# Entry of the gate/up product: x scaled, rounded and split tile by tile, the first three pieces taken by k

## What is computed

```python
x = x + gt_m * (merged @ w_out[l])

h = rms_norm(x, g_ffn_norm[l]) * (1.0 + sc_f) + sh_f
g_ff, u_ff = jnp.split(h @ w_gate_up[l], 2, axis=-1)
x = x + gt_f * ((jax.nn.silu(g_ff) * u_ff) @ w_down[l])
```

## Time and profile before

| | |
|---|---|
| median of 3 runs | 1420.42 us (1415.7 to 1421.6) |
| profiled execution | 1419.05 us |
| its span | 1417.0 us |
| PE busy | 1224.0 us, 86% of the span |
| DVE busy | 921.1 us, 65% |
| ACT busy | 414.4 us, 29% |

### The profile page before, as it was taken

The page is one execution under the profiler, slowest core; times in us unless marked ns, Lnnn a source line. Parts: engine busy times, 40 slices in busy tenths (PEclk is TensorE's granted clock), DMA queues, the critical chain, the costliest instruction groups (busy, mean ns, idle before and its releaser), DMA issues. The chain is left out here.

```text
span 1417.0 us, 20158 instructions
## 1 busy us (share of the span) xinstructions
PE 1224.0 (86%) x7886; PEld 834.8 (59%) x7886; DVE 921.1 (65%) x2035; ACT 414.4 (29%) x882; POOL 276.2 (19%) x264
## 2 busy tenths in 40 slices
PE   4897998878887888888887777889999989899998
PEld 1887867533332424333332222358999669799998
DVE  1594336698787968788786865665556656555542
ACT  2551215311110111111010010244454354544431
POOL 0000000045344444444343444400000000000000
PEclk9899999989999999999999999999999999999999
DMA  9366079599999999999999999973443764344552
GB/s 395 144 238 186 3 282 428 225 408 423 422 420 421 422 421 420 417 419 420 421 400 423 421 401 421 422 316 120 179 170 128 314 280 179 120 179 179 183 207 117
DMA packets 50766, 428.33 MB, mean 302 GB/s; under 512 B 5744, under 2 KB 7920, under 8 KB 8304
## 3 DMA queue, kind: packets, MB, share of 16 engines
q0 software_dynamic: 36864, 268.45, 45.9%
q1 hardware_dynamic: 13808, 158.59, 28.8%
HBM read 423.64 MB, written 1.05 MB: 300 GB/s over the span
## 5 line engine op out<-in xcount | busy, mean ns | idle before, releaser
L1407 PE MATMUL bank<-arena 128*128 128x512 f32 x1024 | 497.1, 614 | 107.3 <-DVE arena L1577 106.8
L1407 PEld LDWEIGHTS bank<-arena 128*128 128x128 f32 x1024 | 176.6, 190 | 408.3 <-DVE arena L1577 271.1
L530 PE MATMUL bank<-rounded,rounded 128*128 128x256 f32 x1288 | 381.0, 296 | 35.6 <-DVE rounded L489 20.6
L1639 DVE CUSTOM_DVE_ANT_0 arena<-arena 128x1024 f32<-128x1024 f32 x256 | 313.4, 1225 | 140.4 <-DMA arena<-experts_in,arena 139.2
L1321 POOL DMA_INDIRECT arena<-experts_in,arena x256 | 275.6, 1077 | 611.6 <-PE bank L1407 352.1
L531 PE MATMUL bank<-rounded,rounded 128*128 128x256 f32 x1288 | 370.6, 288 | 0.0
L532 PE MATMUL bank<-rounded,ring_r 128*128 128x256 f32 x1288 | 369.7, 287 | 0.0
L507 DVE TENSOR_TENSOR ring_r<-ring,rounded 128x1024 fp32r<-128x1024 f32 (+2 forms) x155 | 194.8, 1264 | 143.9 <-ACT rounded L502 142.9
L530 PEld LDWEIGHTS bank<-rounded,rounded 128*128 128x128 f32 x1288 | 252.8, 196 | 44.6 <-issue 32.6
L531 PEld LDWEIGHTS bank<-rounded,rounded 128*128 128x128 f32 x1288 | 252.8, 196 | 3.3 <-issue 2.9
L532 PEld LDWEIGHTS bank<-rounded,ring_r 128*128 128x128 f32 x1288 | 252.9, 196 | 0.0
(11 more groups left out here) (254 smaller groups left out, 946.3 us busy)
## 6 DMA issues: line engine op xcount, KB each, us to landing
ring<-slots_in SPq DMA_DIRECT2D x68, 2048.0 KB, 8.7
arena<-slots_in SPq DMA_DIRECT2D x4, 2048.0 KB, 23.4
arena<-experts_in,arena POOLq DMA_INDIRECT x256, 13.6
xT<-xT_in SPq DMA_DIRECT2D x1, 1024.0 KB, 10.9
mixT<-slots_in SPq DMA_DIRECT2D x1, 1024.0 KB, 13.7
out_dram<-xT SPq DMA_DIRECT2D x1, 1024.0 KB, 3.9
arena<-slots_in SPq DMA_DIRECT2D x1, 896.0 KB, 12.6
uT<-arena SPq DMA_DIRECT2D x4, 142.0 KB, 9.5
```

The costliest lines, as they stand in the source:

```text
L530: pe.matmul(dst, hi[:, k, :], xh, start=(k == 0), stop=False)
L1407: ins = pe.matmul(psum[2 * tt + half][:, :], diag[:, r % DIAGS, :], rows[:, r % GRING, D + 512 * half:D + 512 * half + 512], start=(h == 0 ...
L1639: dve.tensor_tensor_reduce(rows[:, r % GRING, 0:D], rows[:, r % GRING, 0:D], utok[:, tt, :], 1.0, 0.0, ALU.mult, ALU.add, hdot[:, r:r + 1] ...
```

## The change

The third weight split moves from behind the loop of the block before into iteration 4, with the two others behind it. In the gate/up block ACT writes the rounded tile straight from the scaled tile with the shift as its bias, and DVE makes the low part in one operation, (scaled + shift) - rounded, two tiles behind the scaling. The count of low parts rises by one for a tile (eight, where it was four), for which `Split.xcount` is raised by four more. PE takes pieces 0 to 2 together: for each tile k three matmuls for each of the three pieces, into three banks. Later pieces no longer wait for x.

```diff
--- before.py
+++ after.py
@@ -1196,13 +1196,11 @@
                         act.preload_act_table_set("natural_log_exp_and_others")
                     for i in range(len(tiles)):
                         sp3.act_hi(act, i + LEAD)
-                        if following and i in (5, 6):
-                            following.act_prime(act, i - 5, i - 4)
+                        if following and i in (4, 5, 6):
+                            following.act_prime(act, i - 4, i - 3)
                         if squares:
                             act.wait_ge(ev, i + 1)
                             act.activation(uT[:, i, :], xT[:, i, :], ACT.Square).then_inc(nm_sq, 1)
-                    if following:
-                        following.act_prime(act, 2)
 
                 @block.vector
                 def _(dve):
@@ -1214,8 +1212,8 @@
                         sp3.dve_prime(dve, 1)
                     for i, (s, _) in enumerate(tiles):
                         sp3.dve_lo(dve, i + LEAD)
-                        if following and i in (5, 6):
-                            following.dve_prime(dve, i - 5, i - 4)
+                        if following and i in (4, 5, 6):
+                            following.dve_prime(dve, i - 4, i - 3)
                         dve.wait_ge(mm, i + 1)
                         dve.scalar_tensor_tensor(xT[:, i, :], psum[i][:, 0:T], gates[:, i:i + 1], xT[:, i, :],
                                                  ALU.mult, ALU.add).then_inc(ev, 1)
@@ -1223,8 +1221,6 @@
                             dve_add_square(dve, i - 1)
                         if i == len(tiles) - 1 or tiles[i + 1][0] != s:
                             dve.sem_inc(slot_used[(s0 + s) % RING], 1)
-                    if following:
-                        following.dve_prime(dve, 2)
             parts[0] += 1 if squares else 0
 
         eight = [(i // 4, (i % 4) * P) for i in range(8)]
@@ -2148,6 +2144,7 @@
         residual_block("o2", "w_out2", eight, merged, mod2[:, 16:24], (after("w_br"), after("w_out2")), 0, split=o2,
                        following=wgu)
         ffn2_norm = Norm(gain[:, 3, :], mod2[:, 24:32])
+        Split.xcount += KT // 2
         down = residual_split("dn", "w_down", [(i, 0) for i in range(8)], FT, ff, DOWN_AT - 3 * FT * P, width=P, buffers=4,
                               x_split=(ffh, ffl), turn=3)
         with nc.Block() as block:
@@ -2157,18 +2154,32 @@
 
             @block.tensor
             def _(pe):
-                for n in range(4 * NGU):
+                pe.wait_ge(split_lo, wgu.base + LEAD)
+                for k in range(KT):
+                    pe.wait_ge(split_xlo, wgu.xbase + k + 1)
+                    for n in range(LEAD):
+                        hi, lo, dst = wgu.part(n), wgu.weights(n, True), psum[n][:, 0:T]
+                        pe.matmul(dst, hi[:, k, :], wgu.xh[:, k, :], start=(k == 0), stop=False)
+                        pe.matmul(dst, hi[:, k, :], wgu.xl[:, k, :], start=False, stop=False)
+                        ins = pe.matmul(dst, lo[:, k, :], wgu.xh[:, k, :], start=False, stop=(k == KT - 1))
+                        if k == KT - 1:
+                            ins.then_inc(gu_mm, 1)
+                for n in range(LEAD, 4 * NGU):
                     s, j = n // 4, n % 4
                     if s >= 2:
                         if j < 2:
                             pe.wait_ge(gu_act, 2 * (s - 2) + j + 1)
                         else:
                             pe.wait_ge(gu_ev, 2 * (s - 2) + j - 1)
-                    wgu.pe_products(pe, n, psum[n % 8][:, 0:T]).then_inc(gu_mm, 1)
+                    wgu.pe_products(pe, n, psum[n % 8][:, 0:T], wait_x=False).then_inc(gu_mm, 1)
 
             @block.scalar
             def _(act):
-                ffn2_norm.act(act, wgu)
+                ffn2_norm.act_rstd(act)
+                for k in range(KT):
+                    act.wait_ge(nm_n, KT * ffn2_norm.n + k + 1)
+                    act.activation(wgu.xh[:, k, :], uT[:, k, :], ACT.Identity,
+                                   bias=ffn2_norm.shifts[:, k:k + 1]).then_inc(split_xhi, 1)
                 for m in range(4 * NGU):
                     s, j = m // 4, m % 4
                     wgu.act_hi(act, m + LEAD)
@@ -2187,7 +2198,19 @@
 
             @block.vector
             def _(dve):
-                ffn2_norm.dve(dve, wgu)
+                def lower_part(k):
+                    dve.wait_ge(split_xhi, wgu.xbase + k + 1)
+                    dve.scalar_tensor_tensor(wgu.xl[:, k, :], uT[:, k, :], ffn2_norm.shifts[:, k:k + 1], wgu.xh[:, k, :],
+                                             ALU.add, ALU.subtract).then_inc(split_xlo, 1)
+
+                dve.wait_ge(nm_rstd, 2 * ffn2_norm.n + 2)
+                for k in range(KT):
+                    dve.scalar_tensor_tensor(uT[:, k, :], xT[:, k, :], ffn2_norm.gains[:, k:k + 1], ffn2_norm.root,
+                                             ALU.mult, ALU.mult).then_inc(nm_n, 1)
+                    if k >= 2:
+                        lower_part(k - 2)
+                lower_part(KT - 2)
+                lower_part(KT - 1)
                 for m in range(4 * NGU):
                     s, j = m // 4, m % 4
                     wgu.dve_lo(dve, m + LEAD)
```

## The result

| | before | after |
|---|---|---|
| median | 1420.42 us (5 runs, 1415.38 to 1421.6) | 1410.94 us (5 runs, 1407.86 to 1413.56) |
| ratio | 1 | 0.9933, 95% interval 0.9906 to 0.9959 |
| profiled execution | 1419.05 us | 1408.15 us |
| its span | 1417.0 us | 1406.1 us |

A forecast was written before the change was run, and what follows sets the result against it. The prediction took the gate/up and down stages to be bound by PE. Savings of 1.2, 2.2 and 0.5 us sum to 3.9, giving 1416.5 us against the median, range 1412.8 to 1420.0.

The forecast's parts named there:

- Part 1: End of the block before: without the third weight split in its tail, the logarithm comes earlier, 1.2 us saved.
- Part 2: Gate/up entry: x made tile by tile brings the first matmul 1.83 us behind the first scaling, 2.2 us saved.
- Part 3: Behind PE's stop before gate/up: half clock lasts 3.4 us instead of 4.6, 0.5 us saved.
- three stops: PE stops elsewhere of 2.56, 2.88 and 3.09 us, each followed by some 3.4 us at half clock.
- The first rival: Gate/up entry: the clock stays full over the shorter stop, 5.4 us saved in all, 1415.0 us; chance 0.10.
- the fixed 3.4: Block end and gate/up entry: the 1.2 and 2.2 us saved by Part 1 and Part 2.
- Part 4: Gate/up stage: dropped waits and three open banks priced at nothing; piece 4 is ready with some 0.7 us margin.
- the fourth piece in time: Gate/up: low part of the fourth weight made by about 1218.9, needed by PE only near 1222.5.
- The rule that was weighed as a rival: Gate/up: cycling three banks keeps all 72 matmuls at half clock, 1.3 us slower, 1421.7 us; chance 0.04.
- a sign of being wrong: Gate/up: half-clock rows in the middle of the 72 matmuls would show the forecast wrong; no size given.

The follow-up runs named there:

- r2_by_piece: The changed kernel, but PE takes pieces 0, 1, 2 one behind the other, waiting for each tile in piece 0; ratio 0.9977, 1415.78 us.
- r3_waits_kept: The changed kernel, but pieces 3 to 43 keep their four waits for x each; ratio 0.9956, 1413.27 us.
- r1_after: The changed kernel run once more with nothing altered; ratio 0.9958, 1412.49 us.
- r2_warm_before: The kernel before, with 36 matmuls into a free bank in PE's 6.7 us stop ahead of gate/up; ratio 0.9998, 1417.70 us.

## Why the prediction was wrong in size, point by point

**Part 1, the split leaves the tail: right.** 1.17 was forecast and about 1.22 measured, in every kernel with the split moved. The logarithm stands 0.30 behind PE's sum, and the last add came some 0.2 later, where 0.27 was forecast.

**Part 2, x tile by tile: right.** The first matmul was forecast 1.83 behind the first scaling and stands 1.81 behind it; the fused low part takes 0.475 and steps by 0.40, as priced. PE isn't starved, and r2_by_piece shows that this hangs on nine matmuls for a tile.

**Part 3, the clock: the step that failed.** "So I take 3.4 instead of 4.6" made a certainty of three stops, each of which had been seen once. The stop itself was forecast at 3.1 and is 3.08. But behind it the five executions with the new order in full (four of the changed kernel, r3_waits_kept) show no half clock in four cases and 3.4 us in one; with r2_by_piece it is two in six. On average 0.7 to 0.9 us at half stand where 5.1 were: about 4.3 times 0.44 is 1.9 us, not 0.5. The first rival (the clock stays full), which had a chance of 0.10, was the ordinary case.

**The same step left a stop out.** The down entry was priced at nothing, without a reason given; nothing there was changed. The prediction's own rows had a sign of half clock there: 0.98 over the 65 us of the stage. In all four profiles before it ran 3.4 us at half behind its 2.10 us stop; in the changed kernel it does in one of four (with r3_waits_kept one of five). That is 1.45 us in the profiled pair and about 1.2 on average. The two terms together with the fixed 3.4 are 6.5; the means of "total" differ by 224.7 less 218.4, 6.35; the timing by 6.4. The fixed steps are the same in every profile. The two clock terms are averages over four and five profiles, and the weaker one is the down entry, where nothing was changed: the profiles show it, but the timing, good to 1.1, can't tell 6.5 from the 5.3 without it.

**Part 4, the rest: right.** No idle PE up to the down stage, the waits free, the fourth piece in time. The rule that was weighed as a rival, with all 72 matmuls at half clock, didn't come about: in the first profile of the changed kernel 71 of them are recorded at clock 1.00 in 8.60 us over three banks. The Trainium skill, TensorE: Matmul & The Clock Gate, section "A second HAM failure mode: psum-queue depth-cycling", would have had the clock swing there; no trace here shows it. r1_after and r2_by_piece have half clock in the middle of these matmuls, which the prediction had named as a sign of being wrong, but it is one fall and one return. The stops at `o2` and at down, where the order of the matmuls wasn't changed, have such a fall under way too, up to 0.8 us behind the first matmul.

**The median.** The prediction took the saving off the one median of before and allowed 2 to 2.5 us of spread below its first rival; the two medians together used 3.1. With a saving of 6.5 the same sum would have said 1413.9, inside the range and still 3 too high.

**What stays open.** Why the clock falls behind a stop in one execution and not in the next of the same kernel isn't settled, and with it why the new stop of 3.08 us is mostly spared where the one of 2.88 us never was. The down entry had half clock in four of four profiles before, in two of the six with an unfilled stop of 3.08 us at gate/up (r1_after, r2_by_piece), and in none of the three with half of the change or with pairs nor of the two with the filler at gate/up alone. That suggests that it hangs on the moment at which the stages ahead end; this was not tried. The Trainium skill, TensorE: Matmul & The Clock Gate, Part 1, "What's actually happening", says that the chip's look at PE's activity runs freely and isn't tied to the kernel, and so varies the point of change. The spread of these rows agrees with that, but no run here varied the phase on purpose. The shares given, one in five or two in six, rest on few profiles.

## What to carry to other kernels

Judge a small change inside the trace, from a mark just ahead of it to one behind its last effect: here that gave the fixed steps to 0.02 us in one profile, while the code ahead moved by up to 5.4 us from one execution of a kernel to the next. Price the clock behind a stop as a chance, not a number, and do so for every later stop on PE's path, not only the one that was shortened. Where PE must stop anyway, a few idle matmuls into a free bank can keep the clock; in r2_warm_before a third of what they gave went back, since the work behind them wasn't ready at PE's full speed.

## What the runs showed of the hardware that was not expected

- A stop of 3.08 us was followed by no half clock in 4 of 6 profiles, while one of 2.10 us was followed by some 3.3 us of it in 6 of 15 and one of 2.88 us in all 15 where it wasn't filled. The length of a stop alone doesn't decide.
- The same code, up to the first residual add of `o2`, ended anywhere from 1183.2 to 1192.2 us (1181.6 with the filler). Over the executions of the kernel before, a higher mean granted clock goes with a shorter time (correlation -0.75); over the 31 of the changed kernel less so (-0.46). The mean clock was 0.970 before and 0.974 after.
- PE's 164 waits on counts that are already met leave the gate/up stage at the same 127.0 us as without them.
